# Reordering the expert loop of a hybrid decoder step: a first turn of its own, the weightless work between the two up-projections, a bank for each down-projection

## The reference, cut to what matters

```python
logits = x2d @ w_router + b_router            # 288 x 32
top_v, top_i = lax.top_k(logits, 4); gates = softmax(top_v)
# every token goes to its 4 experts; for each expert e and its rows xe:
gu   = xe @ w_up[e] + b_up[e]                 # 1024 -> 2048
gate = minimum(gu[:, :1024], 7.0)
up   = clip(gu[:, 1024:], -7.0, 7.0)
act  = (up + 1.0) * gate * sigmoid(1.702 * gate)
y    = act @ w_down[e] + b_down[e]            # 1024 -> 1024
x   += sum over a token's experts of gates * y
```

## Time and profile before

| | |
|---|---|
| median of 3 runs | 1295.1 us (1292.61 to 1296.22) |
| the profiled execution | 1291.41 us, its span 1289.7 us |
| PE busy, share of the span | 95% |
| DVE, ACT, POOL | 31%, 17%, 6% |
| mean granted TensorE clock | 0.982 |
| read from HBM | 428.91 MB |

### The profile page before, as it was taken

One profiled execution on the slowest core, in us unless ns is written; L12 is line 12 of the kernel. 1 busy time (PEld: TensorE's weight loads), 2 busy tenths in 40 slices (PEclk: granted clock), 3 DMA queues, 4 the chain that ended last, 5 costly groups with the idle time before them and its releaser, 6 DMA issues.

```text
span 1289.7 us, 15534 instructions
## 1 busy us (share of the span) xinstructions
PE 1226.0 (95%) x6160; PEld 601.5 (47%) x6160; DVE 397.4 (31%) x794; ACT 223.2 (17%) x459; POOL 72.3 (6%) x113
## 2 busy tenths in 40 slices
PE   5999999879799999999999999999999999999997
PEld 3777887766534334343433424242433434242433
DVE  2586774533420312212130321212130312212133
ACT  2234333412101011020201101020201111020202
POOL 5001103122200000000000000000000000000000
PEclk9999999879799999999999999999999999999999
DMA  9233110247499999999999999999999999999994
GB/s 272 87 112 104 33 66 1 88 166 244 156 401 425 430 428 428 428 429 427 430 428 429 428 428 428 428 428 429 428 429 428 428 428 428 429 427 429 428 429 166
DMA packets 49670, 434.16 MB, mean 337 GB/s; under 512 B 7166, under 2 KB 13642, under 8 KB 25068
## 3 DMA queue, kind: packets, MB, share of 16 engines
q1 hardware_dynamic: 48508, 430.11, 80.5%
q0 software_dynamic: 1136, 3.71, 1.1%
HBM read 428.91 MB, written 4.88 MB: 336 GB/s over the span
## 4 chain that ended last, share of the span: by engine, by line
PE 74%; DMA 18%; DVE 4%; ACT 1%; issue 1%; POOL 1%; DVEq 0%; SPq 0%; ACTq 0%; POOLq 0%
PE bank L885 27%; DMA ring<-in_w_up 18%; PE bank L904 12%; PE bank L867 7%; PE bank L913 5%; PE bank L536 4%; PE bank L484 3%; PE bank L628 3%; PE bank L818 3%; PE bank L875 2%; PE bank L648 1%; PE bank L685 1%; PE bank L694 1%; PE bank L707 1%; PE bank L692 1%
## 5 line engine op out<-in xcount | busy, mean ns | idle before, releaser
L885 PE MATMUL bank<-ring,xb 128*64 128x512 f32 x2048 | 452.1, 596 | 15.5 <-DMA ring<-in_w_up 15.5
L885 PEld LDWEIGHTS bank<-ring,xb 128*64 128x64 f32 x2048 | 142.8, 137 | 321.1 <-issue 288.6
L1384 DVE TENSOR_TENSOR qkv<-qkv,bank 128x512 f32<-128x512 f32 (+1 forms) x102 | 69.7, 683 | 540.6 <-PE bank L867 540.6
L904 PE MATMUL bank<-ring,zg 128*64 128x512 f32 x1024 | 226.8, 595 | 0.0
L904 PEld LDWEIGHTS bank<-ring,zg 128*64 128x64 f32 x1024 | 70.7, 137 | 131.8 <-issue 127.9
L913 PE MATMUL bank<-zg,ob 128*128 128x128 f32 x816 | 98.5, 278 | 0.0
L867 PE MATMUL bank<-xb,bT 128*128 128x512 f32 (+1 forms) x204 | 97.1, 611 | 1.4 <-ACT xb L1639 1.4
L913 PEld LDWEIGHTS bank<-zg,ob 128*128 128x128 f32 x816 | 95.6, 195 | 0.3 <-issue 0.3
L1368 DVE TENSOR_SCALAR xb<-bank 128x512 f32<-128x512 f32 x32 | 33.4, 1044 | 175.0 <-PE bank L484 175.0
L536 PE MATMUL bank<-hT,ring 128*128 128x288 f32 x320 | 81.0, 414 | 0.0
L1628 ACT ACTIVATE zg<-xb 128x512 f32<-128x512 f32 x32 | 20.2, 632 | 339.5 <-DVE xb L1368 339.5
(11 more groups left out here) (346 smaller groups left out, 882.1 us busy)
## 6 DMA issues: line engine op xcount, KB each, us to landing
ring<-in_w_up SPq DMA_DIRECT2D x128, 2048.0 KB, 21.9
ring<-in_w_down SPq DMA_DIRECT2D x64, 2048.0 KB, 21.5
ring<-in_w_in SPq DMA_DIRECT2D x7, 2048.0 KB, 8.6
ring<-in_w_out SPq DMA_DIRECT2D x2, 2048.0 KB, 7.8
ring<-in_state_gdn SPq DMA_DIRECT2D x4, 512.0 KB, 9.8
out<-ring POOLq DMA_DIRECT2D x1, 2048.0 KB, 12.0
xb<-in_x_prompt SPq DMA_DIRECT2D x1, 1024.0 KB, 5.3
sls<-in_state_gla SPq DMA_DIRECT2D x4, 256.0 KB, 7.0
```

What stands on the lines that cost most here:

```text
L885: last = pe.matmul(bank[2 * q + g][CAP * h:CAP * (h + 1), :], xeT[:, k, q * CAP:(q + 1) * CAP], w[:, kk, g, h, :], start=False, stop=k == ...
L904: last = pe.matmul(bank[5][CAP * h:CAP * (h + 1), :], aT[:, k, CAP * u:CAP * (u + 1)], w[:, k, h, :], start=u == 0 and k == 0, stop=u == 1 ...
L1384: v.tensor_tensor(d, d, bank[banks[at]][0:TN[t], :], ALU.add).then_inc(sems["sc_ok"], 1)
```

## The change

PE's work in the loop is put in another order. The loop's turns from the second on run `up(i,0)`, then all weightless work in one stretch (`mid`: scatter, transposes of `GG`, `act_t` for expert 0, both gathers), then `up(i,1)`, then `downs` (the two down-projections with `act_t` for expert 1 after the first unit). The first turn stands ahead of the loop and runs both ups first, then `mid` and `downs`. Each down-projection and its `act_t` have a bank of their own (5 and 4) and an `aT` buffer of their own. The clamps write in the order they read, and `act_t` reads every fourth column instead. DVE makes `G` a turn earlier, which puts `gates_of(1)` and `token_rows(6)`, with a wait for the first gathers, ahead of the count of rounds. One of the four copies of output rows goes from ACT to DVE. In `gla_level` the loops are turned round, so that blocks of rows 0 to 63 and of rows 64 to 127 alternate.

```diff
@@ gla_level
-                for r in range(2):
-                    rows_ = slice(64 * r, 64 * r + 64)
-                    for t in range(2):
-                        for j in range(2):
-                            m = 2 * t + j
+                for t in range(2):
+                    for j in range(2):
+                        m = 2 * t + j
+                        for r in range(2):
+                            rows_ = slice(64 * r, 64 * r + 64)
                             i = pe.matmul(bank[6 + r][:, m * P:(m + 1) * P], gk[rows_, j, TO[t]:TO[t] + P],
                                           gq[rows_, j, TO[t]:TO[t] + P], start=True, stop=True)
@@ act_t, down (tensor)
-                    last = turn(bank[4][:, j * P:(j + 1) * P], gu[:, 1, j * P:(j + 1) * P], P)
+                    last = turn(bank[5 - q][:, j * P:(j + 1) * P], by_cols(gu[:, 1])[:, :, j], P)
-                            last = pe.matmul(bank[5][CAP * h:CAP * (h + 1), :], aT[:, k, CAP * u:CAP * (u + 1)], w[:, k, h, :],
+                        last = pe.matmul(bank[5 - q][CAP * h:CAP * (h + 1), :], aTs[q][:, k, CAP * u:CAP * (u + 1)], w[:, k, h, :],
@@ the loop (tensor), after
+            def mid(i):
+                pe.wait_ge(sems["yb_ok"], i * 4 + 1)
                 pe.wait_ge(sems["S_ok"], i + 2)
                 scatter(i)
+                pe.wait_ge(sems["G_ok"], i * 2 + 2)
+                for t in range(NTT):
+                    last = turn(bank[4][:, TO[t]:TO[t] + TN[t]], GG[0:TN[t], t, :], TN[t])
+                last.then_inc(sems["p_S"], 1)
+                act_t(0, i * 2 + 1)
+                pe.wait_ge(sems["G_ok"], i * 2 + 3)
+                pe.wait_ge(sems["sc_ok"], i * 6 + 7)
+                gather(0, 7)
+                gather(1, 6)
+            def downs(i):
+                pe.wait_ge(sems["aT_ok"], i * 2 + 1)
+                down(i, 0, 0)
+                pe.wait_ge(sems["S_ok"], i + 3)
+                act_t(1, i * 2 + 2)
+                down(i, 0, 1)
+                pe.wait_ge(sems["aT_ok"], i * 2 + 2)
+                down(i, 1, 0)
+                down(i, 1, 1)
+            pe.wait_ge(sems["xe_ok"], 2)
+            up(0, 0)
+            up(0, 1)
+            mid(0)
+            downs(0)
+            with pe.Fori(1, rounds * PAIRS) as i:
+                pe.wait_ge(sems["xe_ok"], i * 2 + 2)
+                up(i, 0)
+                mid(i)
                 up(i, 1)
+                downs(i)
@@ vector
-                v.tensor_scalar(by_rows(gu[:, 0]), by_cols(bank[2 * q][:]), 7.0, None, ALU.min).then_inc(sems["gu_ok"], 1)
+                v.tensor_scalar(gu[:, 0], bank[2 * q][:], 7.0, None, ALU.min).then_inc(sems["gu_ok"], 1)
...
             token_rows(3)
             gate_rows(1)
+            v.wait_ge(sems["G_ok"], 2)
+            gates_of(1).then_inc(sems["pp_ok"], 1)
+            v.wait_ge(sems["p_gat"], 2)
+            token_rows(6)
             c.done(v.tensor_reduce(cnt[0:1, 0:1], bank[6][0:1, 0:E_N], AX_X, ALU.max), "v_step")
...
+            def next_rows(i):
+                v.wait_ge(sems["p_S"], i + 2)
+                gate_rows(i * 2 + 3)
+                v.wait_ge(sems["G_ok"], i * 2 + 4)
+                gates_of((i + 2) % PAIRS).then_inc(sems["pp_ok"], 1)
+                v.wait_ge(sems["p_gat"], i * 2 + 4)
+                token_rows(i * 3 + 9)
+            swiglu(0, 0)
+            gain(0)
+            v.wait_ge(sems["p_at"], 1)
+            swiglu(0, 1)
+            next_rows(0)
+            rows_out(0)
+            with v.Fori(1, rounds * PAIRS) as i:
                 gain(i)
                 swiglu(i, 0)
+                next_rows(i)
                 v.wait_ge(sems["p_at"], i * 2 + 1)
                 swiglu(i, 1)
+                rows_out(i)
@@ scalar, in the loop
                 sigmoid(i * 2 + 1)
                 act.wait_ge(sems["p_S"], i + 2)
                 act.wait_ge(sems["p_sc"], i * 6 + 6)
-                act.copy(S, bank[6][:, 0:T]).then_inc(sems["S_ok"], 1)
-                turned_act(i * 2 + 1)
+                act.copy(S, bank[4][:, 0:T]).then_inc(sems["S_ok"], 1)
+                turned_act(0, i * 2 + 1)
+                act.wait_ge(sems["p_up"], i * 2 + 2)
                 rows_in(0, 7, i * 2 + 3)
                 sigmoid(i * 2 + 2)
-                rows_out(0, i * 2 + 1)
-                turned_act(i * 2 + 2)
                 rows_in(1, 6, i * 2 + 4)
-                rows_out(1, i * 2 + 2)
+                turned_act(1, i * 2 + 2)
+                rows_out(0, 0, i * 2 + 1)
+                rows_out(0, 1, i * 2 + 1)
+                rows_out(1, 0, i * 2 + 2)
```

More of the change, by code:

```diff
@@ L113, in program @@
         zf = zg[:].rearrange("p a b -> p (a b)")
-        aT = cut(zf, 0, 4, P)
+        aTs = [cut(zf, 0, 4, P), cut(hTf, 512, 4, P)]
         sg = cut(zf, 512, 512)
@@ L887, in up, with act_t, down @@
                     last.then_inc(sems["w_used" if u < 3 else "p_up"], 1)
-            def act_t(w):
+            def act_t(q, w):
                 pe.wait_ge(sems["act_ok"], w)
                 for j in range(4):
-                    last = turn(bank[4][:, j * P:(j + 1) * P], gu[:, 1, j * P:(j + 1) * P], P)
+                    last = turn(bank[5 - q][:, j * P:(j + 1) * P], by_cols(gu[:, 1])[:, :, j], P)
                 last.then_inc(sems["p_at"], 1)
[L896 to L903, removed]
-                            last = pe.matmul(bank[5][CAP * h:CAP * (h + 1), :], aT[:, k, CAP * u:CAP * (u + 1)], w[:, k, h, :],
-                                             start=u == 0 and k == 0, stop=u == 1 and k == 3, skip_group_check=True)
-                    last.then_inc(sems["w_used" if u < 1 else "p_yd"], 1)
+            def down(i, q, u):
+                n = 8 + 2 * q + u
+                pe.wait_ge(sems[f"ld_w{n % 6}"], i * 32 + 32)
+                w = slot[WSLOT[n % 6]].rearrange("p (k h n) -> p k h n", k=4, h=2)
+                for k in range(4):
+                    for h in range(2):
+                        last = pe.matmul(bank[5 - q][CAP * h:CAP * (h + 1), :], aTs[q][:, k, CAP * u:CAP * (u + 1)], w[:, k, h, :],
+                                         start=u == 0 and k == 0, stop=u == 1 and k == 3, skip_group_check=True)
+                last.then_inc(sems["w_used" if u < 1 else "p_yd"], 1)
             def gather(j, b):
@@ L930, in _ @@
             rounds = pe.value_load(rnd[0:1, 0:1], min_val=1, max_val=5)
-            with pe.Fori(0, rounds * PAIRS) as i:
-                pe.wait_ge(sems["xe_ok"], i * 2 + 2)
-                up(i, 0)
+            def mid(i):
                 pe.wait_ge(sems["yb_ok"], i * 4 + 1)
@@ L936, in _ @@
                 scatter(i)
-                up(i, 1)
[L939 to L957, removed]
+                pe.wait_ge(sems["G_ok"], i * 2 + 2)
[25 more added lines that the diff above has]
+                mid(i)
+                up(i, 1)
+                downs(i)
             total = rounds * PAIRS
@@ L1367, in swiglu @@
                 v.wait_ge(sems["p_up"], i * 2 + at)
-                v.tensor_scalar(by_rows(gu[:, 0]), by_cols(bank[2 * q][:]), 7.0, None, ALU.min).then_inc(sems["gu_ok"], 1)
-                v.tensor_scalar(by_rows(gu[:, 1]), by_cols(bank[2 * q + 1][:]), 7.0, -7.0, ALU.min, ALU.max).then_inc(sems["gu_cl"], 1)
+                v.tensor_scalar(gu[:, 0], bank[2 * q][:], 7.0, None, ALU.min).then_inc(sems["gu_ok"], 1)
+                v.tensor_scalar(gu[:, 1], bank[2 * q + 1][:], 7.0, -7.0, ALU.min, ALU.max).then_inc(sems["gu_cl"], 1)
                 v.wait_ge(sems["gu_ok"], i * 2 + at)
@@ L1376, in swiglu, with rows_out @@
                 pick_gu(q, (i + 1) % PAIRS * 2 + q)
+            def rows_out(i):
+                v.wait_ge(sems["p_yd"], i * 2 + 2)
+                v.tensor_copy(yr[CAP:2 * CAP, 512:D], bank[4][CAP:2 * CAP, :]).then_inc(sems["yb_ok"], 1)
             def gain(w, ats=range(6), banks=(6, 7, 6, 7, 6, 7)):
@@ L1427, in _ @@
             rounds = v.value_load(rnd[0:1, 0:1], min_val=1, max_val=5)
-            with v.Fori(0, rounds * PAIRS) as i:
+            def next_rows(i):
[12 more added lines that the diff above has]
+            with v.Fori(1, rounds * PAIRS) as i:
                 gain(i)
                 swiglu(i, 0)
-                v.wait_ge(sems["p_gat"], i * 2 + 2)
-                gates_of((i + 1) % PAIRS).then_inc(sems["pp_ok"], 1)
-                token_rows(i * 3 + 6)
+                next_rows(i)
                 v.wait_ge(sems["p_at"], i * 2 + 1)
                 swiglu(i, 1)
-                v.wait_ge(sems["p_S"], i + 2)
-                gate_rows(i * 2 + 3)
+                rows_out(i)
             total = rounds * PAIRS
@@ L1628, in sigmoid, with turned_act, rows_out @@
                 act.activation(sg, gu[:, 0], ACT.Sigmoid, scale=1.702).then_inc(sems["sig_ok"], 1)
-            def turned_act(w):
+            def turned_act(q, w):
                 act.wait_ge(sems["p_at"], w)
-                act.copy(aT.rearrange("p a b -> p (a b)"), bank[4][:]).then_inc(sems["aT_ok"], 1)
-            def rows_out(q, w):
```

(5 more changed lines are left out.)

## The result

The changed kernel takes 1339.55 us (median of four runs, 1336.32 to 1341.81) against 1294.44 us (1292.61 to 1296.22): a ratio of 1.0345 [1.0312, 1.0378]. 1341 us was predicted. Its profiled execution took 1337.3 us with a span of 1335.6 us, 45.9 us more than the span before (1289.7).

What follows compares the result with a forecast made beforehand. Weights bound the kernel, PE having 2.1 us to spare per turn; the change makes PE the bound. 23.2 + 21.3 + 3.0 + 4.0 + 0.7 + 0.5 - 2.7 - 0.6 = +49.4 on 1291.4 gives 1341 us, range 1316 to 1352.

Steps and rivals of the forecast that it cites:

- The wait: In mid, PE idles 2.86 us per turn ahead of act_t(0) for DVE's swiglu product; +23.2 us over 15 turns.
- PE above the weights: In the loop, PE's turn grows from 56.65 to 59.51 us, above the weights' 58.73, so PE is the bound.
- The clock: Behind the new idle in each of 15 turns, a lowered PE clock costs 1.42 us; +21.3 us (0 to 21.3).
- a clock that holds: Rival: the idle in the loop doesn't lower the clock; 1320 us, or 1317 with a free strided load; chance 0.20.
- The strided load: In act_t, loading every fourth column is slower; +3 us taken, between nothing and 8.4 us.
- The start: Ahead of the loop, late states cost +4.0 us and faster gla_level gives -2.7 us.
- GLA: Ahead of the loop, eight gla_level calls take 1.30 us instead of 1.64; -2.7 us (0 to 6.6 saved).
- The first turn: Longer idle ahead of it prolongs the low clock, +0.7 us; loop entry behind it, +0.5 us.
- The tail: At the kernel's end, one copy of the last output rows moves from ACT to DVE; -0.6 us.
- The dry stretches: In the first two turns the DMAs run dry a few us; nothing if PE is the bound, several us otherwise.
- The rival in which the weights set the pace: act_t(0) waits under 2.1 us, turns stay 58.73, loop end gives -4.8: 1287 us; chance 0.12, of which 0.07 faster.
- Its second form: Weights set the pace, but the first turns' dry DMA stretches cost several us: 1294 us, no change; chance 0.05.

Runs made afterwards that it cites:

- the wait filled: Changed kernel with three matmuls of unused result put ahead of act_t(0): 1315.65 us, ratio 1.0142.
- the first experiment: Changed kernel with both gathers put ahead of act_t(0) in mid, nothing else moved: 1295.92 us, ratio 1.0011.
- one loop: The kernel of the first experiment without the first turn written apart, all 16 turns in the loop: 1296.07 us, ratio 1.0025.
- the old clamps: Changed kernel with the strided clamps and the contiguous act_t transposes put back: 1356.34 us, ratio 1.0464.
- without the late start: The kernel of the first experiment with DVE's count of rounds and last states again ahead of its wait for the first gathers: 1295.04 us, ratio 1.0008.

## Why the prediction was right

- *The wait.* Forecast 2.86 us in each of 15 turns, measured 2.95, at the place and by the releaser named. Both the steps (last addition, clamps of 0.675 us, product) and the cover of 0.54 us came out of the earlier trace rows. The gathers, moved ahead of it, take it away; moved alone into before, it appears.
- *PE above the weights.* That the first 2.1 us of the wait are free was the margin of the earlier trace rows; 59.70 us with the wait filled and, with the low clock, 61.3 us are above 58.73, and no wait for the weights is left.
- *The clock.* 1.42 us per turn were taken from one stretch ahead of the loop, with 0.20 for a clock that holds. It fell in each of the loop's turns, for 1.48 us in the mean. That stretch had cost more than was taken, 1.72 us with its bias matmuls (1.36 us for 1.06 at full clock), so that 1.42 came this near is in part luck. The filled wait, 24 us faster, shows that the idle is the cause, and not the new order of the matmuls.
- *The strided load.* 3 us taken, about 3 us found. The factor of 1.5 from DVE's writes held for the load itself, 210 ns for 140, but most of it lies beside matmuls: four loads are 0.28 us longer, the four transposes of an `act_t` only 0.09 (0.75 for 0.66). That the load must become slower is what the Trainium skill (SBUF — State Buffer, Door 1: The DMA port swizzle) says, and the trace agrees for the load; the 8 us of time that I had drawn from it are not there.
- *The start: the one term with the wrong sign.* +4.0 - 2.7 = 1.3 us later were forecast, 3.95 earlier were found. The delay itself was right: from the gathers' end to the bias matmul 6.02 us for 2.53, +3.5 us. GLA gave 4.4, not 2.7: L760, the row that I took for like, gave a factor of 1.26, L648 one of 1.5. The Trainium skill (TensorE: Matmul & The Clock Gate, Part 3: Packing small matmuls — row/col tiling) has matmuls on different groups of rows run at the same time, by which I had estimated a factor of 2; the trace lies halfway. Some 3 us remain, and the windows show a likely place for them: from 220 to 230 us the granted clock was 0.77 in before and 1.00 in after. That they come from there is not shown.
- *The first turn* cost 0.3 us, not 0.7 + 0.5: the bias matmuls were slower (2.08 us for 1.36) and the 64 instructions behind them faster (14.72 for the 15.30 of the earlier trace rows), together only 0.14 us more, in spite of the longer idle. The entry of the loop doesn't show at all. *The tail*: -0.5 for -0.6.
- *The dry stretches* are where they were expected (116 GB/s at 430 to 440 us), and cost nothing while PE is the bound. When the weights are the bound, as in the first experiment, 7.5 us of lost transfers stand beside a loop that is 6.2 us longer than before.
- *The rival in which the weights set the pace* had a step that fails: -4.8 us at the loop's end. In the first experiment, where the weights do set the pace in the new order, PE works 42.1 us from the last wait for weights to the end of the loop (1240.48 to 1282.5), before 41.7 (1233.67 to 1275.40). The last unit to land wasn't what PE waited for last. Its second form, 1294 us, stands near the 1295.92 that were measured, but by terms that cancel: the spans of before and of that experiment differ by +0.9 us at the start, +6.2 in the loop and -0.5 in the tail, and the form had +1.3, -4.8 with several us for the dry stretches, and -0.6.

So the sum was close in part because its one wrong term is small beside 44.5 us of wait and clock. Span against span it was +45.9 us for +49.4: the 15 turns grew by 50.0 us for 23.2 + 21.3 + 3.0 = 47.5, and the start and the first turn fell by 3.6 where +2.5 was forecast. That 1341 lies within 1.5 us of the median is partly luck. Left open: what the later states cost at the end of the kernel, and why the clock ahead of the loop differs.

## What to carry to other kernels

Work that "needs no weights" isn't free to stand together: ask of each moved instruction which chain on another engine it waits for, what covered that chain before, and which independent work is queued behind it; here, with two gathers put ahead of a wait of 2.95 us, 44 us came back. An idle of PE can cost twice, as here, some 20 us by itself and 24 by the clock after it; of the first, only the part above PE's spare time per turn counts. Run the parts alone: the one small edit that the change's name doesn't mention, an order of three loops, made the kernel faster (0.995), and the new order of the expert loop, even with its wait covered and with that edit in it, did not (1.0011).

## What the runs showed of the hardware

An idle of PE of 1.89 us once per turn was followed by 1.2 GHz in 13 of 15 turns, one of 2.95 us in all; idles of up to 1.24 us in before lowered nothing. What decides between these lengths is not shown. Three useless matmuls in the idle made the kernel 24 us faster.

The same code ahead of the loop ends at different times: the first bias matmul stood at 343.61 us in after, 343.75 with the filled wait, 343.47 in one loop, 345.66 with the old clamps and 348.49 with the gathers first, and none of these edits touches what runs before 320 us. PE is busy all of the time from 200 to 210 us in each; what differs is the granted clock, 0.62 in the window of the first experiment above and 1.00 in that of after:

```profile
200.00:210.00 10.00, 10.00 (x59) 7.45 (x60) 3.12 (x3) 2.57 (x4) 4.86 (x3) 1.00 0.01 2
```

So a difference of 5 us in one profiled execution says nothing here of an edit, and the medians with and without the late start (1295.92 and 1295.04) don't settle its 3.5 us either.
